# A hybrid three-block kernel: which side of each weight split the side work of VectorE stands on

## The reference

```python
# block 1
proj = x @ w_in                       # q, k, v and gates of three branches
ya = gated_linear_attention(...)      # 4 heads, chunked, with a decay per channel
yb = sliding_window_attention(...)    # 16 heads of 64
yc = block_attention(...)             # 8 heads of 128
merged = sum(sigmoid(gate_b) * (y_b @ w_branch_b)); out = layer_norm(ALPHA * x + merged @ w_o)
# block 2: wide depthwise convolution and gated delta rule, then w_out, SwiGLU, w_down
# block 3: mLSTM (6 heads), differential attention (4), attention with top-64 keys (6),
#          then w_out, relu(x @ w_up)**2 @ w_down
```

## Time and profile before

| | us |
|---|---|
| median of three runs | 3479.57 |
| the profiled execution, its own time | 3477.05 |
| its span | 3475.0 |
| PE busy | 3401.7 (98%) |
| DVE busy | 2221.7 (64%) |
| ACT busy | 1631.1 (47%) |
| mean granted clock of TensorE | 0.991 |

### The profile page before, as it was taken

The page is one execution under the profiler, slowest core; times in us unless marked ns, Lnnn a source line. Parts: engine busy times, 40 slices in busy tenths (PEclk is TensorE's granted clock), DMA queues, the critical chain, the costliest instruction groups (busy, mean ns, idle before and its releaser), DMA issues.

```text
span 3475.0 us, 50561 instructions
## 1 busy us (share of the span) xinstructions
PE 3401.7 (98%) x20360; PEld 3029.2 (87%) x20360; DVE 2221.7 (64%) x2880; ACT 1631.1 (47%) x1924; POOL 6.3 (0%) x9
## 2 busy tenths in 40 slices
PE   8999999999999999999999999999999999999997
PEld 8998998888889999878888888799999788888886
DVE  6777555555568997665555566767666644456666
ACT  4445544444434443544444455543444444555554
POOL 0000000000000000000000000000000000000000
PEclk9999999999999999999999999999999999999999
DMA  6454566666655522555555565545446466565554
GB/s 193 148 167 152 155 194 199 195 199 202 215 162 161 157 86 74 190 161 184 191 189 188 188 211 194 174 154 164 148 146 210 152 194 191 187 204 196 194 193 147
DMA packets 324179, 608.84 MB, mean 175 GB/s; under 512 B 28253, under 2 KB 42591, under 8 KB 322728
## 3 DMA queue, kind: packets, MB, share of 16 engines
q1 hardware_dynamic: 317640, 587.45, 53.2%
q10 hardware_dynamic: 6368, 19.01, 1.4%
HBM read 604.29 MB, written 2.10 MB: 175 GB/s over the span
## 4 chain that ended last, share of the span: by engine, by line
PE 93%; DVE 4%; ACT 1%; issue 1%; DMA 0%; SPq 0%; ACTq 0%; DVEq 0%
PE ps L593 21%; PE ps L594 21%; PE ps L595 21%; PE ps L615 16%; PE ps L621 8%; DVE xtok L1782 1%; DVE arena L1782 1%; DVE arena L1776 1%; PE ps L1071 1%; DVE w_lo L1776 1%; DMA ring<-in_w_in 0%; PE ps L1090 0%; PE ps L772 0%; ACT w_hi L1254 0%; PE ps L1087 0%
## 5 line engine op out<-in xcount | busy, mean ns | idle before, releaser
L1776 DVE TENSOR_TENSOR w_lo<-ring,w_hi 128x1024 fp32r<-128x1024 f32 (+2 forms) x1136 | 1366.3, 1209 | 1018.1 <-ACT w_hi L1254 837.0
L1254 ACT ACTIVATE w_hi<-ring 128x1024 fp32r<-128x1024 f32 (+2 forms) x1136 | 1182.7, 1047 | 1536.8 <-PE ps L593 1151.2
L593 PE MATMUL ps<-x_both,w_hi 128*128 128x256 f32 x2368 | 684.0, 289 | 0.8 <-DVE w_lo L1776 0.8
L594 PE MATMUL ps<-x_both,w_hi 128*128 128x256 f32 x2368 | 672.2, 284 | 0.0
L595 PE MATMUL ps<-x_both,w_lo 128*128 128x256 f32 x2368 | 672.1, 284 | 0.0
L615 PE MATMUL ps<-x_both,w_hi 128*128 128x512 f32 x2432 | 612.3, 394 | 0.6 <-DVE w_lo L1776 0.5
L615 PEld LDWEIGHTS ps<-x_both,w_hi 128*128 128x128 f32 x2432 | 439.1, 190 | 79.9 <-issue 0.9
L593 PEld LDWEIGHTS ps<-x_both,w_hi 128*128 128x128 f32 x2368 | 456.3, 193 | 6.2 <-issue 5.7
L594 PEld LDWEIGHTS ps<-x_both,w_hi 128*128 128x128 f32 x2368 | 456.6, 193 | 0.7 <-issue 0.5
L595 PEld LDWEIGHTS ps<-x_both,w_lo 128*128 128x128 f32 x2368 | 456.1, 193 | 0.0
L621 PEld LDWEIGHTS ps<-x_both,w_lo 128*128 128x128 f32 x2432 | 332.6, 191 | 23.9
(11 more groups left out here) (352 smaller groups left out, 3222.0 us busy)
## 6 DMA issues: line engine op xcount, KB each, us to landing
ring<-in_w_in SPq DMA_DIRECT2D x416, 512.0 KB, 3.5
ring<-in_w_down SPq DMA_DIRECT2D x216, 512.0 KB, 4.6
ring<-in_w_gate_up SPq DMA_DIRECT2D x176, 512.0 KB, 4.4
ring<-in_w_up SPq DMA_DIRECT2D x128, 512.0 KB, 4.2
ring<-in_w_out SPq DMA_DIRECT2D x64, 512.0 KB, 4.6
ring<-in_w_branch SPq DMA_DIRECT2D x36, 512.0 KB, 4.0
ring<-in_w_in SPq DMA_DIRECT2D x48, 384.0 KB, 3.1
ring<-in_w_o SPq DMA_DIRECT2D x32, 512.0 KB, 4.8
```

Of the source, the lines that this page charges most:

```text
L593: first = pe.matmul(out, left[0], right[0], start=start, stop=False)
L594: pe.matmul(out, left[0], right[1], start=False, stop=False)
L1254: last = act.activation(w_hi[:, s, :, 0:width], ring[:, s, :, 0:width], ACT.Copy)
L1776: return dve.tensor_tensor(o, a, b, op)
```

## The change

Two `next(side)` calls in VectorE's `splits` trade their conditions. Where a step is drawn once a chunk (the first and third block), the step now comes behind the split of chunk c + 3 instead of ahead of it. Where two steps are drawn for a chunk (the second block) there is still one on each side.

```diff
@@ def splits(sec, u, it, hidden=False, before=None, side=None, every=1, halves=False):
                 for c in range(AHEAD, AHEAD + sec.chunks):
                     if before is not None:
                         before(c - AHEAD)
-                    if side is not None and (c - AHEAD) % every == every - 1:
+                    if halves and side is not None:
                         next(side)
                     split(sec.chunk(u, c), sec.more(it), c % sec.chunks * CH if hidden else None)
-                    if halves and side is not None:
+                    if side is not None and (c - AHEAD) % every == every - 1:
                         next(side)
```

## The result

The changed kernel takes 3506.25 us (median of four runs, 3503.81 to 3506.95), the kernel before beside it 3479.70 us (3477.05 to 3479.93). The ratio is 1.0076, with a 95% interval from 1.0063 to 1.0087: slower by 26.55 us. The prediction said 3506.5 us, in a range from 3497 to 3517. The profiled execution took 3507.15 us, its span 3505.1 us, which is 30.1 us more than the span before.

A forecast was written before the change was run, and what follows sets the result against it. PE's own stream plus its waits was taken as the bound. Stalls of 12.3 and 11.65, less 0.1, plus 4.1 for the clock made 28.0 us on 3477.05, so 3505.0 (median 3507.6); stated 3506.5, range 3497 to 3517.

The forecast's parts named there:

- Part one: First block's eight levels and diagonal: PE stalls behind a split put in front of each step, 12.3 us in sum.
- Part two: Third block: the same sum at twelve places, 2.15 us at the logits, 2.95 at the gate values, 11.65 in all.
- Part three: Splits and SyncE's loads in the first and third block start no later: a gain of 0.2 us at most.
- Part four: TensorE's clock behind stalls of 2 us and more: 2.4 drops, 4.1 us, between none (0) and six (10).
- The sum: Whole kernel: 12.3 + 11.65 - 0.1 + 4.1 = 28.0 us slower.
- Only the first block: Rival: only the first block's chained levels pay, the third block's delays may cover each other; some 15 us, 3493 us; 7 in 100.
- The clock at every stall: Rival: the clock drops at each of twelve stalls over a microsecond; 44 us, 3522 us; 5 in 100.
- The ring takes it up: Rival: the splits run ahead and PE never sees the late step; 0 to -0.4 us, 3479 us; 5 in 100.

The follow-up runs named there:

- the second profile: The changed kernel run again with nothing altered, one look for the clock: 3505.72 us, span 3503.6 us.
- the two half changes: The kernel before with the new order in the first block alone, 3489.67 us, and in the third block alone, 3491.33 us.
- the fifth kernel: The kernel before, with TensorE's side step drawn one chunk later in the first and third block: 3475.46 us, ratio 0.9993.
- the third kernel: The changed kernel, with TensorE's side step drawn one chunk later in the first and third block: 3476.01 us, run again 3475.96 us.

## Why the prediction was right, point by point

**Part one, the levels.** Predicted 1.74, 1.52, 2.13, four times 1.26, 0.30 and 1.57, in sum 12.3. Measured 1.68, 1.51, 2.10, 1.24, 1.24, 1.41, 1.24, 0.28 and 1.44, in sum 12.14. The formula (split waits for ACT, ACT for PE, then 1.14, the weights and the hop) holds at each to 0.15 us, and the price does repeat: the waits don't shrink from level to level, since the chain that delays PE starts at PE. The later steps of the first block cost nothing, as I took them.

One reading in it was wrong. I took the 0.24 us between DVE and PE at the third level for the hop, but PE was not waiting there: its row at 120.58 in the earlier trace rows has no idle time. It had waited at the first level, where DVE's last instruction and PE's start are

```profile
99.59 0.68 DVE L1776 TENSOR_TENSOR arena<-arena 128x512 f32<-128x512 f32 x1
100.39 2.05 PE L903 MATMUL ps<-arena 128*128 128x128 f32 x16 [0.24 <-DVEq L2262]
```

and 100.39 - 100.28 = 0.11 us is the hop, as at every level of the changed kernel. So the third level had 0.13 us of slack, and the formula's 0.24 is too much by 0.13 at each place. A term that the formula lacks makes up for it: a level's 16 matmuls take 2.05 us behind a wait (139.22 above) and 1.95 without one. That the formula comes as near as 0.02 us at the regular levels is in this part luck.

**Part two, the third block.** Predicted 11.65, measured 12.45. The logits came at 2.18 for 2.15. The miss is in the gate values: I took 3.45 and then 0.5 off, because ACT's gate work would not be late with PE. It was. ACT of the changed kernel at this place:

```profile
2322.82 1.06 ACT L1254 ACTIVATE w_hi<-ring 128x1024 fp32r<-128x1024 f32 x1 [2.95 <-PE ps L593]
...
2326.16 1.04 ACT L1254 ACTIVATE w_hi<-ring 128x1024 fp32r<-128x1024 f32 x1
...
2331.66 0.20 ACT L1361 ACTIVATE small<-small 128x2 f32<-128x2 f32 x1
2331.77 1.04 ACT L1254 ACTIVATE w_hi<-ring 128x1024 fp32r<-128x1024 f32 x1
```

DVE, the split in front of the gate values:

```profile
2332.84 1.23 DVE L1776 TENSOR_TENSOR w_lo<-ring,w_hi 128x1024 fp32r<-128x1024 f32 x1 [3.21 <-ACT w_hi L1254]
```

PE, held meanwhile:

```profile
2330.96 0.28 PE L595 MATMUL ps<-x_both,w_lo 128*128 128x256 f32 x1
2334.41 0.39 PE L826 MATMUL ps<-small,upper 128*128 128x6 f32 x2 [3.17 <-DVE small L1779]
```

From 2322.82 to 2332.81 ACT works without a gap, and its run begins with a split that PE let go. The same run of ACT in the kernel before began so:

```profile
2303.20 1.06 ACT L1254 ACTIVATE w_hi<-ring 128x1024 fp32r<-128x1024 f32 x1 [2.42 <-PE ps L593]
```

That is 19.62 us earlier. The split at 2332.84 stood at 2313.29 before, 19.55 us earlier, while PE's last matmul ahead of line 826 stood at 2311.34 and is 19.62 us later. So ACT had taken over PE's delay whole, there was no 0.5 to take off, and the 3.45 of the formula was the right size: 3.43. By my own argument of part one, that ACT is as late as PE, I should not have taken it off.

The other places agree within 0.3 us, but for line 882, where 0.1 and 0.55 were predicted and about 0 and 1.10 measured. The trace puts 0.8 us of that to a wait for DVE; the rest is not settled.

**Part three, no gain.** There was none: the 0.2 us at `w_lo` stands in the list as before.

**Part four, the clock.** Predicted 2.4 drops, 4.1 us, at stalls of 2 us and more. The profiled execution lost 6.0 us, the second profile 4.3 (73.8 against 65.2 us at the lower clock). Of the three stalls that I had named, two were followed by a drop, line 826 and the logits, in four profiles of four; the third, at the third level, never was, though it is the costliest of the first block (2.10 us). The first level, which I had not named, had a drop in one profile of the three with these waits. I had not foreseen that drops far away move as well. The one at 1427.7 came in seven of ten profiles, with one wait of 3.4 us in all of them; the two behind the one-column matmuls of line 873 came in seven and in three of ten. So the 4.1 came out near, but partly by luck: it is a balance of drops won and lost that no step of mine had counted.

The Trainium skill, in "TensorE: Matmul & The Clock Gate", section "HAM oscillation — how this bites in real kernels", allows no drop for stalls of this length. The rows 2335.70 and 2458.50 above, at 0.50 and 0.51 behind waits of 3.2 and 1.9 us, do not agree with it, and the measurement decides. By that rule the sum would have been 24.0 us, which is too little by some 4.6 us for the second profile, at 28.6 us over the span before.

**The sum.** Stalls 24.6 for 23.95 (23.85 with the 0.1 us of gain), the clock 4.3 to 6.0 for 4.1. The profiled execution came out 2.1 us above the 3505.0 that the sum gave. For the median the sum gave 3507.6; I said 3506.5 and gave no reason for the 1.1 us between. That the median then came out at 3506.25, within 0.3 us, is luck: the terms are good to a microsecond or two, and so is the median.

**The rivals.** "Only the first block" (3493) falls with the two half changes. "The clock at every stall" (3522) falls with the levels: of seven waits one was followed by the lower clock, in one profile of three. "The ring takes it up" (3479) names the right condition, slack over 3.1 us, which the kernel does not have. Where it was given (4.73 us at the fourth level of the fifth kernel), that case became true: 3476 us. The order did change, as the timelines show.

## What to carry to other kernels

When two streams of work share an in-order engine, the one whose consumer has the least slack goes first, and slack is read in the timeline as the distance from the producer's last end to the consumer's start, less the hop between them (0.11 us here), place by place and not as a mean of busy shares. An instruction moved ahead costs its own wait as well as its time. If that wait hangs on the engine that is being delayed, the cost does not wear off: it is paid again at every place. It can be bought back on the consumer's side, by taking up the result one step later.

## What was not expected of the hardware

- The drops of TensorE's clock are not fixed to places. The changed kernel with the same waits showed 77.1 us at 1.2 GHz in one execution and 73.8 in another, and a drop of 6.8 us in the second block came in seven of ten profiles behind an unchanged wait of 3.4 us. So single profiles differ by 1.5 to 3 us for this alone. They are not loose either: two profiles of the third kernel showed the same seven drops.
- A stall of 1.9 us at the logits was followed by the lower clock in all four profiles that have it. At the first level one of 1.9 us was so once in three, at the third level one of 1.84 us never. The length of the wait alone does not decide; what does was not separated here.
- The clock also fell behind matmuls of one column though PE had hardly waited: at 2481.3 and 2576.9 us in the kernel before, with PE busy for 3.31 and 3.37 of the 3.40 us ahead (line 873). These came in seven and in three of the ten profiles.
- The hop from DVE's last instruction to PE is 0.11 us wherever PE waited for a level, before and after.
